# The expert layer of a float32 model in eleven blocks of 128 routed tokens, with the tokens stationary and the weights moving

## The chip, the cores and the metric

The kernel runs on one core of a Trainium2 chip. TensorE multiplies matrices, VectorE (DVE) and ScalarE (ACT) work on vectors, SyncE (SP) issues most DMAs. Each engine takes its instructions in order; semaphores tie the engines together. The metric is the time of one execution on the device in microseconds (us), as the median of several runs.

## The reference

The reference runs a two-layer hybrid mixer model and a two-layer diffusion trunk one after the other, all in float32, on 256 tokens of width 1024 (and 256 context tokens in the second half). The change touches one part alone, the mixture of experts in the second layer of the first half:

```python
def moe_swiglu(h, router_w, w1, w3, w2):
    logits = (h @ router_w).astype(F32)
    top_v, top_i = lax.top_k(logits, TOP_K)                 # TOP_K = 2
    probs = jax.nn.softmax(top_v, axis=-1)
    gates = jnp.sum(jax.nn.one_hot(top_i, N_EXPERTS, dtype=F32) * probs[..., None], axis=-2)
    out = jnp.zeros_like(h)
    for e in range(N_EXPERTS):                              # N_EXPERTS = 8
        out = out + gates[..., e:e + 1] * swiglu(h, w1[e], w3[e], w2[e])
    return out                                              # w1, w3: 1024 x 1408, w2: 1408 x 1024
```

Each of the 256 tokens picks two of eight experts, so the layer needs 512 token-expert pairs, while computing every expert for every token makes 2048. `swiglu(h, w1, w3, w2)` is `(silu(h @ w1) * (h @ w3)) @ w2`.

## The kernel before

The residual X lies in SBUF with features on partitions (8 tiles of 128 features x 256 tokens). A float32 product is made of three float32r passes: every operand is split into a high part (rounded to float32r) and a low part (the rest), and `passes()` (lines 606 to 608) does high*high, high*low and low*high into one PSUM bank. ACT makes the high part of a weight tile (line 1173), DVE the low part (line 1576). Products whose operands are plain float32 (the router, the spreading of one row over all partitions) are single calls; the program turns each into two instructions, a high and a low one, so the trace has two records for each.

A feed-forward layer is a loop (`ffn`, line 719) whose turn has 30 units. Units 0 to 21 make 128 hidden features each (8 tiles of the input width, three passes each, weights stationary, 256 tokens moving); units 22 to 29 make 128 output features each (11 hidden tiles, three passes). For the experts the loop has eight turns, one for each expert, over all 256 tokens, and the output of a turn is multiplied by the expert's gates (`expert_gates`, line 1683) before it goes into X (line 1640). Beside it each turn makes 3 column tiles of the second half's modulation (lines 634 and 641: 8 calls of 384 columns and 3 of 2 columns, which are 16 and 6 records).

Weights go through three raw buffers (`RAW`, filled by SP in `load_ffn`, 1 MB or 1.4 MB each) and three split buffers (`WS`). SP issues the load of a raw buffer when the split of its last contents is done; ACT splits unit n when PE has done unit n-3. All orders are written out by hand, engine by engine, and the waits are semaphore waits in the code.

Ahead of the expert loop stand the norm, the split of the normed h (`norm_apply`), the router (PE line 986), the top two and their softmax (DVE lines 1985 to 1998), and the spreading of the gates over all partitions (PE line 997, DVE line 2003). During this the weights of the first units are already in SBUF. Behind the loop stand the final norm of the first half and the norm of the second half's first layer.

## Time and profile before

| what | value |
|---|---|
| median of the runs | 3401.73 us (3401.4 to 3408.96, three runs) |
| the profiled execution, its own time | 3409.84 us |
| its span, first to last instruction | 3408.1 us |
| granted TensorE clock, mean over the span | 0.966 |
| PE busy, share of the span | 94% |
| DVE busy, ACT busy | 46%, 38% |
| DMA, mean over the span | 150 GB/s, 512 MB |

The span is cut into 40 slices of 85 us on the page. PE is busy in nearly all of them, and the chain of waits that ended last runs over PE for 87% of the span. A busy PE is no PE at its peak: the records of matmuls overlap, so what one costs in a stream is read from the distance between the starts of two neighbours, not from its duration.

### The profile page before, as it was taken

How to read it: one execution, taken by the hardware profiler on the slowest of the kernel's cores; microseconds unless marked ns; L12 is line 12 of the kernel's file. 1: busy time of each engine (PE TensorE's matmuls, PEld its weight loads, DVE VectorE, ACT ScalarE, POOL GpSimd, SP SyncE). 2: the span in 40 equal slices, each digit the busy share in tenths (PEclk: the TensorE clock that was granted, in tenths of full speed). 3: DMA queues.
4: the chain of work that ended last, by engine and by line, in shares of the span. 5: the costliest groups of instructions: out<-in, count | busy, mean ns of one | idle time of the engine just before them, and what ended most of it. 6: DMA issues, size and time to landing. Idle time of an engine off the chain costs nothing.

```text
span 3408.1 us, 53358 instructions
## 1 busy us (share of the span) xinstructions
PE 3200.0 (94%) x20698; PEld 2771.3 (81%) x20698; DVE 1563.7 (46%) x2328; ACT 1308.2 (38%) x1942; POOL 0.2 (0%) x4
## 2 busy tenths in 40 slices
PE   7998989899999999998999999999999999989899
PEld 5887888789999999996777777778777777777798
DVE  4553446545555555554232345533334232346555
ACT  4353343533444434444222244432223222245444
POOL 0000000000000000000000000000000000000000
PEclk8999999889999999998999999999999999999899
DMA  8748764346666666563635322144452545522454
GB/s 298 238 127 263 198 198 136 100 123 181 187 180 198 182 172 186 178 188 109 205 87 170 126 59 75 50 122 132 112 154 75 168 136 155 171 63 87 114 176 133
DMA packets 680961, 512.09 MB, mean 150 GB/s; under 512 B 14795, under 2 KB 674702, under 8 KB 680598
## 3 DMA queue, kind: packets, MB, share of 16 engines
q1 hardware_dynamic: 601510, 390.56, 39.4%
q10 hardware_dynamic: 79216, 118.01, 10.9%
q8 instruction: 195, 3.19, 0.4%
q14 instruction: 40, 0.33, 0.0%
HBM read 507.46 MB, written 1.05 MB: 149 GB/s over the span
## 4 chain that ended last, share of the span: by engine, by line
PE 87%; ACT 5%; DVE 3%; issue 2%; DMA 2%; SPq 1%; ACTq 0%; DVEq 0%
PE bank L606 26%; PE bank L608 25%; PE bank L607 25%; PE bank L634 3%; ACT ring L1227 2%; DMA ada_halves<-in_ada_w 1%; PE bank L641 1%; PE bank L1125 1%; PE bank L1116 1%; ACT weights_split L1173 1%; DVE weights_split L1576 1%; PE bank L1137 1%; ACT hn_split L1226 1%; ACT hn_split L1234 1%; PE bank L690 0%
## 5 line engine op out<-in xcount | busy, mean ns | idle before, releaser
L606 PE MATMUL bank<-hn_split,weights_split 128*128 128x256 f32 (+1 forms) x3888 | 1281.2, 330 | 104.7 <-issue 37.3
L607 PE MATMUL bank<-hn_split,weights_split 128*128 128x256 f32 (+1 forms) x3888 | 1252.4, 322 | 0.0
L608 PE MATMUL bank<-hn_split,weights_split 128*128 128x256 f32 (+1 forms) x3888 | 1251.7, 322 | 0.0
L1576 DVE TENSOR_TENSOR weights_split<-weights_raw,weights_split 128x1024 fp32r<-128x1024 f32 (+2 forms) x670 | 873.2, 1304 | 275.5 <-ACT weights_split L1173 272.6
L1173 ACT ACTIVATE weights_split<-weights_raw 128x1024 fp32r<-128x1024 f32 (+2 forms) x670 | 748.1, 1118 | 603.0 <-PE bank L608 583.9
L606 PEld LDWEIGHTS bank<-hn_split,weights_split 128*128 128x128 f32 x3888 | 757.0, 195 | 238.1 <-issue 139.0
L607 PEld LDWEIGHTS bank<-hn_split,weights_split 128*128 128x128 f32 x3888 | 757.6, 195 | 65.8 <-issue 18.0
L608 PEld LDWEIGHTS bank<-hn_split,weights_split 128*128 128x128 f32 x3888 | 756.8, 195 | 52.2
L1662 DVE TENSOR_TENSOR ring<-ring,bank 128x256 f32<-128x256 f32 (+1 forms) x198 | 101.0, 510 | 998.4 <-PE bank L608 874.9
L606 PE MATMUL bank<-hidden_split,weights_split 128*128 128x256 f32 (+1 forms) x1584 | 508.6, 321 | 0.0
L607 PE MATMUL bank<-hidden_split,weights_split 128*128 128x256 f32 (+1 forms) x1584 | 505.1, 319 | 0.0
L608 PE MATMUL bank<-hidden_split,weights_split 128*128 128x256 f32 (+1 forms) x1584 | 505.0, 319 | 0.0
L1262 ACT ACTIVATE hidden_split<-ring 128x256 fp32r<-128x256 f32 (+1 forms) x198 | 96.9, 490 | 606.3 <-DVE ring L1662 606.2
L606 PEld LDWEIGHTS bank<-hidden_split,weights_split 128*128 128x128 f32 x1584 | 302.5, 191 | 32.4 <-issue 11.9
L608 PEld LDWEIGHTS bank<-hidden_split,weights_split 128*128 128x128 f32 x1584 | 302.5, 191 | 20.9
L607 PEld LDWEIGHTS bank<-hidden_split,weights_split 128*128 128x128 f32 x1584 | 302.6, 191 | 19.8
L1259 ACT ACTIVATE ring<-bank 128x256 f32<-128x256 f32 (+1 forms) x198 | 90.0, 454 | 470.6 <-PE bank L608 470.2
L1640 DVE SCALAR_TENSOR_TENSOR residual<-bank,half_gate,residual 128x256 f32<-128x256 f32 x112 | 49.8, 480 | 232.3 <-PE bank L608 232.2
L1672 DVE TENSOR_TENSOR hidden_split<-ring,hidden_split 128x256 fp32r<-128x256 f32 (+1 forms) x198 | 100.5, 508 | 0.0
L1200 ACT ACTIVATE ring<-residual 128x256 f32<-128x256 f32 (+1 forms) x160 | 73.9, 464 | 48.6 <-DVE residual L1640 43.6
L634 PE MATMUL bank<-ada_halves,cond_second_padded 128*32 128x384 f32 x768 | 81.8, 498 | 0.0
L1600 DVE TENSOR_TENSOR rstd<-rstd,ring 128x256 f32<-128x256 f32 (+1 forms) x144 | 71.6, 497 | 3.9 <-ACT ring L1200 3.3
(300 smaller groups left out, 1957.2 us busy)
## 6 DMA issues: line engine op xcount, KB each, us to landing
weights_raw<-in_moe_w SPq DMA_DIRECT2D x176, 512.0 KB, 5.2
weights_raw<-in_w_ffn_in SPq DMA_DIRECT2D x176, 512.0 KB, 5.1
ada_halves<-in_w_ada ACTq DMA_DIRECT2D x96, 768.0 KB, 4.8
ada_halves<-in_ada_w ACTq DMA_DIRECT2D x54, 768.0 KB, 4.9
weights_raw<-in_w_in SPq DMA_DIRECT2D x60, 512.0 KB, 4.9
weights_raw<-in_moe_w SPq DMA_DIRECT2D x32, 768.0 KB, 4.5
weights_raw<-in_w_ffn_out SPq DMA_DIRECT2D x32, 768.0 KB, 4.6
weights_raw<-in_ffn_w SPq DMA_DIRECT2D x44, 512.0 KB, 5.5
```

What stands on the lines that cost most here:

```text
L606: mm(ps, wh, xh, start=first, stop=False)
L607: mm(ps, wh, xl, start=False, stop=False)
L608: return mm(ps, wl, xh, start=False, stop=last)
L634: i = mm(PS[bank][32 * j:32 * j + 32, 0:ADA_COLS], condp[:, 4 * h + j, :], AH[:, h, j, :], start=h == 0, stop=h == 1)
L1173: act.activation(split_view(slot, 0, kts, n), raw, ACT.Copy).then_inc(split_high, 1)
L1200: act.activation(square_tile(m, T)[:, seg], X[:, m, 0:T][:, seg], ACT.Square).then_inc(square_ready, 1)
L1259: act.activation(RING[:, 0, 0:T], PS[0][:, 0:T], ACT.Silu).then_inc(drained[0], 1)
L1262: act.activation(gs(0, T)[:, f, :], RING[:, 1, 0:T], ACT.Copy).then_inc(g_high, 1)
L1576: tt(split_view(slot, 1, kts, n), raw, split_view(slot, 0, kts, n).bitcast(F32), ALU.subtract)\
L1600: tt(RS[:, 0:T], RS[:, 0:T], square_tile(m, T), ALU.add).then_inc(square_added, 1)
L1662: tt(RING[:, 1, 0:T], RING[:, 0, 0:T], PS[1][:, 0:T], ALU.mult).then_inc(drained[1], 1)
L1672: tt(gs(1, T)[:, f, :], RING[:, 1, 0:T], gs(0, T)[:, f, :].bitcast(F32), ALU.subtract)\
```

## The change

The expert layer leaves the loop. The router gives each token its two experts; a counting step with small matmuls gives each token-expert pair a slot so that each expert owns whole blocks of 128 slots. Eleven blocks always suffice (`MOE_BLOCKS = (2*256 - 8)//128 + 8`), and eleven are always computed. For each block:

- `gather`: 32 float32r matmuls of 128 columns with 0/1 selection matrices (`PICK`) pick the block's tokens out of token rows and leave them with features on partitions; ACT and DVE split them (`XB`).
- `up`: 16 units of one row tile (128 input features) of w1 or w3, all 1408 columns moving, in chunks of 512, 512 and 384, with the block's 128 tokens stationary. Three passes each. The units alternate between w1 (banks 0 to 2) and w3 (banks 3 to 5).
- `turn`: silu on ACT, the product on DVE, 11 PE transposes, copies by ACT. Between the first four transposes and the rest stands `scatter` of the block before.
- `down`: 11 hidden tiles by two halves of 512 output columns in plain float32 (no split), the hidden tile stationary, w2 moving from its own buffers (`W2R`, four pairs of row tiles). Inside it stand the sum of the slots' gates and the next block's `gather`.
- `scatter`: 16 float32r matmuls of 256 columns put the gated result back to token columns, and DVE adds it to X, eight adds for each block.

The expert's number is read by SP from SBUF for each block, and the weight loads take their address from it. The whole is written out, eleven times, with no loop on any engine. All weights of a block are loaded for the block: 17.3 MB, also where two blocks have one expert or a block is empty.

```diff
+MOE_BLOCKS = (2 * SEQ - EXPERTS) // P + EXPERTS
+UP_CHUNKS = ((0, 512), (512, 512), (1024, 384))
+            def load_experts():                                     # SP
+                def up_tile(b, k):
+                    kk = KT * b + k
+                    sp.wait_ge(split_both, MOE_U + 2 * max(0, kk - 2))
+                    r, s = slice(k * P, (k + 1) * P), (MOE_B + kk) % 3
+                    sp.dma_start(RAW[:, s, 0:FFN_GROUP], a["moe_w1"][0][expert[b]][r, :]).then_inc(raw_full[s], 16)
+                    sp.dma_start(RAW[:, s, FFN_GROUP:], a["moe_w3"][0][expert[b]][r, :]).then_inc(raw_full[s], 16)
+                def down_pair(b, j):
+                    n, q = DOWN_PAIRS * b + j, min(2, GT - 2 * j)
+                    if n >= W2_PAIRS:
+                        m = n - W2_PAIRS
+                        sp.wait_ge(S["moe_down"], GT * (m // DOWN_PAIRS) + min(2 * (m % DOWN_PAIRS) + 2, GT))
...
+                sp.wait_ge(S["moe_routed"], BLOCKED)
+                for b in range(MOE_BLOCKS):
+                    expert[b] = sp.value_load(BLOCK_EXPERT[0:1, b:b + 1], min_val=0, max_val=EXPERTS - 1)
+                    up_tile(b, 0)
+                    if b:
+                        down_pair(b - 1, 4)
+                        down_pair(b - 1, 5)
...
-            load_ffn("ffn1.1")
+            load_experts()
+            def experts():                                          # PE
+                def gather(b):
+                    pe.wait_ge(S["moe_picked"], 2 * (b + 1))
+                    for half in range(2):
+                        for k in range(4 * half, 4 * half + 4):
+                            for n in range(4):
+                                t, part = n // 2, n % 2
+                                i = mm(PS[half][:, k % 4 * P:(k % 4 + 1) * P], HROW[:, part, t, k * P:(k + 1) * P],
+                                       PICK[b % 2][:, t, :], start=n == 0, stop=n == 3)
...
+                def up(b):
+                    for v in range(UP_UNITS):
+                        n, k, w = UP_UNITS * b + v, v // 2, v % 2
...
+                        pe.wait_ge(split_both, MOE_U + n + 1)
+                        for c, (c0, cn) in enumerate(UP_CHUNKS):
+                            ps = PS[3 * w + c][:, 0:cn]
+                            xh, xl = (XB[b % 2][:, part, k, :] for part in (0, 1))
+                            wh, wl = (up_split(n, part)[:, c0:c0 + cn] for part in (0, 1))
+                            mm(ps, xh, wh, start=k == 0, stop=False)
+                            mm(ps, xl, wh, start=False, stop=False)
+                            i = mm(ps, xh, wl, start=False, stop=k == KT - 1)
...
+                def scatter(b, banks):
+                    pe.wait_ge(S["moe_y_split"], 2 * (b + 1))
+                    pe.wait_ge(S["moe_placed"], b + 1)
+                    for q in range(4):
+                        if q >= 2 and banks[q] == banks[q - 2]:
+                            pe.wait_ge(x_updated, x0 + KT * b + 2 * (q - 1))
...
+                for b in range(MOE_BLOCKS):
+                    up(b)
+                    turn(b)
+                    down(b)
+                scatter(MOE_BLOCKS - 1, (2, 3, 0, 1))
...
+                def split_up(n):                                    # ACT; DVE makes the low part
+                    block = MOE_B + n // 2
+                    act.wait_ge(raw_full[block % 3], 32 * (block // 3 + 1))
+                    act.wait_ge(unit_done, MOE_U + n - 2)
+                    act.activation(up_split(n, 0), up_raw(n), ACT.Copy).then_inc(split_high, 1)
...
-                            if moe:
-                                tmp = RING[:, 2 + m % 2, 0:T]
-                                dve.wait_ge(x_updated, g * 8 + (x0 + m - 1))
-                                tt(tmp, src[:, 0:T], GATES[:, g, :], ALU.mult).then_inc(gated, 1)
-                                dve.wait_ge(gated, g * 8 + (4 + m + 1))
-                                residual(m, 0, tmp, gate(m, 0), g * 8 + (x0 + m - KT + 1))
...
+                for b in range(MOE_BLOCKS):                         # DVE
+                    for v in range(3, UP_UNITS):
+                        split_up(UP_UNITS * b + v)
+                    if b + 1 < x.n_turns:
+                        add_modulation(b + 1)
+                    for c, (c0, cn) in enumerate(UP_CHUNKS):
+                        dve.wait_ge(S["moe_silu"], 3 * b + c + 1)
...
+                        tt(HID[:, c0:c0 + cn], HID[:, c0:c0 + cn], PS[3 + c][:, 0:cn], ALU.mult).then_inc(S["moe_hidden"], 1)
+                    if b + 1 < MOE_BLOCKS:
+                        pick(b + 1)
+                    if b:
+                        for k in range(KT):
+                            dve.wait_ge(S["moe_scattered"], 4 * (b - 1) + k // 2 + 1)
+                            residual(k, 0, PS[2 + k // 2 % 2][:, k % 2 * SEQ:(k % 2 + 1) * SEQ], gate(k),
+                                     x0 + KT * (b - 2) + k + 1 if b > 1 else None)
+                    if b + 1 < MOE_BLOCKS:
+                        split_up(UP_UNITS * (b + 1))
+                        block_low(b + 1)
+                        split_up(UP_UNITS * (b + 1) + 1)
+                        split_up(UP_UNITS * (b + 1) + 2)
+                    place(b)
```

PE before, inside a turn, from the last pass of the hidden features to the first two products of the output (weights_split is the stationary tile; 128x256 is what moves):

```order
L608 MATMUL bank<-hn_split,weights_split 128x256
L735 ISA
L612 REGISTER_ALU
L616 REGISTER_ALU
L606 MATMUL bank<-hidden_split,weights_split 128x256
L607 MATMUL bank<-hidden_split,weights_split 128x256
L608 MATMUL bank<-hidden_split,weights_split 128x256
```

The hidden features are ready for the next product as they stand, so nothing lies between the two halves of a turn.

PE in the changed kernel, from the last passes of block 1's `up` (lines 901 to 903) to the first of block 2's. block_split is the block's tokens, block_pick and block_place the selection matrices of gather and scatter, block_hidden the hidden rows, block_out_split the block's result; the numbers are those of the two buffers:

```order
L903 MATMUL bank<-weights_split,block_split_114 128x384
L929 MATMUL bank<-tables,block_hidden 128x128 x4
L945 MATMUL bank<-block_place_122,block_out_split 128x256 x16
L929 MATMUL bank<-tables,block_hidden 128x128 x7
L955 MATMUL bank<-expert_down,block_hidden_turned 128x512 x10
L965 MATMUL bank<-small,block_pick_125 128x1 x2
L955 MATMUL bank<-expert_down,block_hidden_turned 128x512 x2
L880 MATMUL bank<-block_pick_124,token_rows_split 128x128 x32
L955 MATMUL bank<-expert_down,block_hidden_turned 128x512 x10
L901 MATMUL bank<-weights_split,block_split_113 128x512
```

Transposes, scatter and gather are new on PE; the down products are 22 calls in place of 264 passes of half the width.

SP before, where the expert loop begins (one raw buffer is filled by two DMAs of 128x8x128):

```order
L557 UNCONDITIONAL_BRANCH
L557 ISA
L564 ISA
L564 DMA weights_raw<-in_moe_w 128x8x128
L565 DMA weights_raw<-in_moe_w 128x8x128
L561 REGISTER_ALU
```

SP in the changed kernel, where block 1 begins:

```order
L654 TENSOR_LOAD block_expert
L654 ISA x2
L639 ISA
L639 DMA weights_raw<-in_moe_w 128x1408
L640 DMA weights_raw<-in_moe_w 128x1408
L649 ISA
L649 DMA expert_down<-in_moe_w 128x2x1024
L649 ISA
L649 DMA expert_down<-in_moe_w 128x1024
L639 ISA
L639 DMA weights_raw<-in_moe_w 128x1408
L640 DMA weights_raw<-in_moe_w 128x1408
```

The loads of w2 (line 649) stand in the one queue between those of w1 and w3 (lines 639 and 640), so that the second row tile of a block is issued behind two loads that wait for the block before to use its w2.

## Rows read from the trace of the kernel before

**Rows 1.** The page: span, busy time, the chain's shares by engine.
```profile
span 3408.1 us, 53358 instructions
PE 3200.0 (94%) x20698; PEld 2771.3 (81%) x20698; DVE 1563.7 (46%) x2328; ACT 1308.2 (38%) x1942; POOL 0.2 (0%) x4
...
PE 87%; ACT 5%; DVE 3%; issue 2%; DMA 2%; SPq 1%; ACTq 0%; DVEq 0%
```

**Rows 2.** Busy time in stretches of the expert layer; columns as the header says.
```profile
core 0: us, PE busy (x) PEld busy (x) DVE busy (x) ACT busy (x) POOL busy (x), PEclk, DMA share, GB/s
640.00:706.00 66.00, 47.04 (x285) 43.44 (x284) 34.77 (x84) 26.36 (x45) 0.00 (x0) 0.72 0.29 81
...
914.00:1018.00 104.00, 98.68 (x815) 96.53 (x816) 57.10 (x78) 43.75 (x61) 0.00 (x0) 1.00 0.65 186
```

**Rows 3.** Timeline of PE at both ends of the loop: start, duration, line, [idle before].
```profile
707.36 0.55 PE L606 MATMUL bank<-hn_split,weights_split 128*128 128x256 f32 x1 [1.88 <-DVE cond_second_padded L1727]
707.71 0.41 PE L607 MATMUL bank<-hn_split,weights_split 128*128 128x256 f32 x1
707.92 0.41 PE L608 MATMUL bank<-hn_split,weights_split 128*128 128x256 f32 x1
...
1533.67 0.50 PE L682 MATMUL bank<-tables,rstd 128*128 128x2 f32 x4
```

**Rows 4.** Timeline of PE at the edge of two turns.
```profile
810.27 0.36 PE L606 MATMUL bank<-hn_split,weights_split 128*128 128x256 f32 x1 [1.59 <-issue]
814.88 0.28 PE L606 MATMUL bank<-hn_split,weights_split 128*128 128x256 f32 x1 [2.58 <-issue]
```

**Rows 5.** Timeline of PE: neighbouring float32r passes of 256, then of 512 columns.
```profile
636.03 0.28 PE L606 MATMUL bank<-hn_split,weights_split 128*128 128x256 f32 x1
636.15 0.28 PE L607 MATMUL bank<-hn_split,weights_split 128*128 128x256 f32 x1
...
1640.04 0.39 PE L608 MATMUL bank<-hn_split,weights_split 128*128 128x512 f32 x1
...
1641.40 0.39 PE L608 MATMUL bank<-hn_split,weights_split 128*128 128x512 f32 x1
```

**Rows 6.** Plain float32 calls: one line's records (ns, first to last start), and timeline.
```profile
L882 PE MATMUL bank<-ret_out,tables x4: 590/592/594, 598.9 to 600.2; 128*128 128x512 f32 x4
...
2105.58 2.08 PE L1116 MATMUL bank<-mla_k,mla_q 96*128 96x512 f32 x4
2107.49 1.06 PE L1125 MATMUL bank<-mla_sum_diagonals,mla_probs 128*128 128x128 f32 x8
2108.48 1.09 PE L1137 MATMUL bank<-mla_probs_t,mla_v 128*64 128x128 f32 x16
```

**Rows 7.** Transposes: one line's records (ns, first to last start).
```profile
L800 PE MATMUL bank<-tables,context_rows x16: 272/272/332, 57.7 to 59.4; 128*128 128x128 f32 x16
```

**Rows 8.** Groups of instructions by form, whole span: busy us, mean ns, idle before.
```profile
L1576 DVE TENSOR_TENSOR weights_split<-weights_raw,weights_split 128x1408 fp32r<-128x1408 f32 x144 | 233.9, 1624 | 51.7 <-ACT weights_split L1173 51.6
L1173 ACT ACTIVATE weights_split<-weights_raw 128x1408 fp32r<-128x1408 f32 x144 | 198.1, 1376 | 282.6 <-PE bank L608 281.8 <-issue 0.6
L634 PE MATMUL bank<-ada_halves,cond_second_padded 128*32 128x384 f32 x768 | 81.8, 498 | 0.0
L1259 ACT ACTIVATE ring<-bank 128x512 f32<-128x512 f32 x66 | 39.4, 597 | 243.0 <-PE bank L608 243.0
L1662 DVE TENSOR_TENSOR ring<-ring,bank 128x512 f32<-128x512 f32 x66 | 45.4, 688 | 540.6 <-PE bank L608 504.0 <-ACT ring L1259 36.6
L1640 DVE SCALAR_TENSOR_TENSOR residual<-ring,mod_first,residual 128x256 f32<-128x256 f32 x64 | 31.0, 485 | 6.5
```

**Rows 9.** DMA: a stretch of pure loading (columns of rows 2), and time to landing.
```profile
15.00:25.00 10.00, 7.00 (x38) 3.30 (x42) 2.52 (x7) 3.57 (x7) 0.00 (x0) 0.66 1.05 387
...
weights_raw<-in_moe_w SPq DMA_DIRECT2D x176, 512.0 KB, 5.2
```

**Rows 10.** Timeline ahead of the loop: last add to X, norm, router, top two.
```profile
665.53 0.48 DVE L1640 SCALAR_TENSOR_TENSOR residual<-bank,mod_first,residual 128x256 f32<-128x256 f32 x1 [0.16 <-PE bank L608]
...
677.88 13.82 PE L986 MATMUL bank<-router_w,hn_split 128*128 128x8 f32 x64 [8.98 <-DVE hn_split L1622]
```

**Rows 11.** Timeline of DVE at the loop's end: the last add to X.
```profile
1534.42 0.48 DVE L1640 SCALAR_TENSOR_TENSOR residual<-ring,mod_first,residual 128x256 f32<-128x256 f32 x1
```

**Rows 12.** A small DVE operation of 128 columns: one line's records.
```profile
L2150 DVE TENSOR_SCALAR mla_sum_diagonals<-tables,small x48: 285/286/290, 2101.9 to 3149.8; 128x128 f32<-128x128 f32 x48
```

More of the change, by code:

```diff
@@ L345, in program @@
             phase(f"ffn1.{layer}")
-            loop_blocks(2 if layer == 0 else EXPERTS)
+            if layer == 0:
+                loop_blocks(2)
+            else:
+                for n in range(KT * MOE_BLOCKS):
+                    blocks.append(None)
+                    units.extend([(len(blocks) - 1, None, None, None, None)] * 2)
         for layer in range(DEPTH):
@@ L1710, in out_phase @@
                 for u in range(u0, u1):
[L1711 removed]
+                    ahead(u, u1 + (0 if name in ("out1.1", "out2.1") else 2))
                     m = u - u0
```

477 lines of the change are left out of this document (382 added, 95 removed).

## The prediction

> **What bounds the kernel now.** I read the page first: over the whole span PE is busy for 94%, and the chain that ended last runs over PE for 87% [rows 1]. DVE (46%) and ACT (38%) are covered by it. The second view is the busy time by stretches. In one turn of the expert loop PE is busy for 98.7 of 104 us at a granted clock of 1.00, DVE for 57, ACT for 44, and the DMA engines for 0.65 at 186 GB/s [rows 2]. So the layer costs what its stream of passes on PE costs, until something else is put in its way. The timeline of PE gives its length: the first product starts at 707.36 and the norm behind the last one at 1533.67, so 826.3 us for eight turns, 103.3 each [rows 3]. Neighbouring passes of 256 columns start 0.120 us apart [rows 5], and a turn has 22 x 8 x 3 + 8 x 11 x 3 = 792 of them: 95.0 us. The modulation beside them costs 8 x 2 records of 384 columns (on 32 of the array's columns; 16 records busy 81.8 / 768 x 16 = 1.7 us [rows 8]) and six small ones, some 0.7, so 2.4 us. At the edge of two turns PE stands still for 1.59 and 2.58 us on "issue" [rows 4], 4.2 us. That is 101.6 of 103.3.
>
> **The price of a pass in the changed shape.** A float32r pass of 512 columns costs (1641.40 - 1640.04) / 6 = 0.227 us [rows 5], less than two of 256. For 384 columns there is no row; I take the middle of 0.120 and 0.227, 0.174. A plain float32 call of 512 columns is two records, and four records of line 882 start within 1.3 us, 0.43 apart; four of line 1116 take 1.91 us to the next line's start, 0.478 each [rows 6]. So a call costs 0.86 to 0.96 us, and I take 0.86, from the line with 128 rows and 128 columns, as here. Transposes: 16 in 1.7 us of starts, 0.113 [rows 7].
>
> **One block on PE.**
> - up: 16 units x (6 x 0.227 + 3 x 0.174) = 16 x 1.88 = 30.1 us.
> - turn: 11 transposes x 0.12 = 1.3; scatter 16 x 0.12 (256-column passes) = 1.9.
> - down: 22 x 0.86 = 18.9 us (bound above 22 x 0.96 = 21.0). In float32r it would be 66 passes x 0.227 = 15.0, so this part of the change costs PE 4 us per block and spares ACT and DVE the splits.
> - the gates' sum, four records: 0.5.
> - gather: 32 passes of 128 columns. No row shows a float32r pass so narrow. From below: eight float32 records of 128 columns start in 0.99 us, 0.12 each [rows 6], the same as a float32r pass of 256, so something beside the columns keeps records 0.12 apart. From above: float32 takes two records, 0.24. I take 0.12, the nearest in kind (one record each): 3.8 us; the other end is 7.7.
>
> **What PE waits for in a block.** In turn PE waits inside scatter. DVE has to do the three products of the hidden rows (0.69, 0.69, 0.55), the four selections (0.29 each [rows 12]) and then the adds to X (0.48 each [rows 8]), and scatter's third pair needs the first two adds, since it reuses banks 2 and 3. Counted from the end of up: products done at 0.95, selections at 2.1, two adds at 3.1, third pair 3.2 to 3.7, two more adds at 4.1, fourth pair to 4.7, seven transposes to 5.5. PE's own work in it is 3.2, so 2.3 to 2.4 us of idle; silu (0.6 each, as line 1259 [rows 8]) is hidden by the last unit, because it starts on w1's banks a unit earlier. At the end of down no wait is left: the next unit 0 uses other banks, and its 1.88 us cover the split of the result (0.6 + 0.7 behind the last half), for which unit 1 waits.
>
> Split weights: a unit of 1408 columns costs ACT 1.376 and DVE 1.624 [rows 8]. DVE alone could feed one unit in 1.68; the ring of three gives a period of (1.38 + 1.62 + 0.35 of hand-overs + 1.88) / 3 = 1.74. Both are under PE's 1.88, so PE keeps the lead, with little to spare. The one thing in ACT's way is the issue of two modulation loads (some 1 us) in seven blocks; I give it 4 us in all.
>
> Raw weights: a block loads 3 x 1024 x 1408 x 4 bytes = 17.3 MB. The trace's stretch of pure loading ran at 387 GB/s with the engines full [rows 9]: 44.6 us, and the block is 58.9. The average fits, the order does not quite. A row tile of w1 and w3 is 1.44 MB, 3.7 us at 387; the loop now lands 2 x 0.5 MB 5.2 us after issue [rows 9], of which the bytes are 3.7 at 186 / 0.65 = 286 GB/s, so some 1.5 us are latency, and a tile lands 5.2 to 5.9 us after its two issues. Issue waits for the split of the tile three before. Landing to both splits done takes 1.38 + 2 x 1.62 + 0.3 = 4.9. So three tiles pass in 10.1 to 10.8, and PE takes 11.3 for three. Into this the queue puts w2's fourth pair (1.05 MB, 2.7 us) behind tile 5, and tiles 6 and 7 come some 2.5 us late. I take 2 us per block, between 0 and 5.
>
> A block: 30.1 + 3.2 + 2.4 + 18.9 + 0.5 + 3.8 = 58.9, with the loads 60.9. Eleven: 670. Less the first scatter and last gather (5.7), plus 7 modulation parts of 2.4 (17) and ACT's 4: 685. The loop was 826.3: -141 us. With it go 264 passes a turn in down, the 33 us of issue at turn edges, and DVE's gate products, which were covered.
>
> The Trainium skill, page "DMA: Bandwidth & Descriptors", section "Where 436 GB/s comes from", gives a core some 358 GB/s from HBM as the side that binds. This case's stretch went faster, 387, so the measurement decides; by the page a block's loads take 48.3 us and the late tiles grow by about 1.4 us a block, 15 us in all.
>
> **Ahead of the blocks.** The last add to X starts at 665.53 and the first product at 707.36 [rows 3, 10]. What goes: the split of h, 64 router records at 0.216 (13.8 us [rows 10]), the spreading of the gates. What comes: h, 16 transposes and 32 router records, some 10.4 us at that rate, to 680; top two for both halves at once, 2.5; counting matmuls and seven small DVE steps to the experts' numbers, about 687; and only then may SP read and load, a row tile after 6 to 7 us. Meanwhile slots, selections, gather(0) at the slow rate (7 us), its splits, and the first weight split: first product about 701.5, and the splits of units 1 to 3 stand in one queue with other DVE work, 2 us more. I take -4 us, between -10 and +8. The loads, ready in advance before, are hidden behind gather.
>
> **Behind them.** Before, the last add to X started 0.75 us after PE's next work [rows 11]. Now, after the last down: the split of the result 1.6, two splits for the next layer on DVE 2.5, then eight adds and seven sums of squares in turn, 7 us. That is 11 for 1.3: +10.
>
> Sum: -141 - 4 + 10 = -135. The profiled execution took 3409.8 us (span 3408.1), which gives 3275; it lies 8 above the median of 3401.7. On the median: 3267 us.
>
> **Rivals.**
> - R1, the narrow passes of gather cost as float32: +0.12 x 32 = 3.8 us in ten blocks, 38: 3305. For it: the passes are of a width that no row has. Against: one record should not cost two.
> - R2, late tiles cost 5 us a block, not 2 (the queue's waits on moe_down add up): +33, 3300. For it: 10.8 against 11.3 leaves half a us in a cycle.
> - R3, the idle of turn drops the clock. At half clock a pass of 256 costs 0.21 [rows 3]. For it: PE pauses in every block's turn. Against: after pauses of 1.59 and 2.58 us the next pass at 814.88 had the full-clock duration of 0.28 [rows 4]. If it fell in each block and three to five us of down ran at half speed, +30: 3297. The Trainium skill's "TensorE: Matmul & The Clock Gate", section "HAM oscillation — how this bites in real kernels", says that kernels with thin M, waiting for DMA between short bursts, fall to the half clock again and again; this block of 128 tokens is such a shape, and the trace agrees only for the longer idle ahead of 707.36.
> - R4, slower than before: the loads pace the blocks. The turn before moved 186 GB/s [rows 2]; if one in-order queue with its waits on moe_down got no more, a block would take 17.3 / 0.186 = 93 us and the kernel 3267 + 11 x 32 = 3619. It decides from the block time that eats the gain, 60.9 + 135 / 11 = 73.2 us, 236 GB/s. Against: 387 was reached, the engines' share now is 0.65, and a queue of 1.4 MB requests has a tile or two in flight.
> - R5, better than said: no late tiles and half the idle in turn, -22 - 13: 3232.
>
> **Numbers.** Forecast 0.50 (own range 3240 to 3290), R1 0.22, R2 0.12, R3 0.04, R5 0.08, R4 0.04. Range 3228 to 3322: R1, R2, R3 and R5 with their spread; out of it stay R4 and the cases where R1 and R2 meet. What a measurement of this kernel can tell from no change is about 0.3%, 10 us. All but R4 are faster by far more: faster 0.95, same 0.01, slower 0.04.
>
> **What would show it.** Starts of 512-column passes in up 0.227 apart; plain float32 records in down 0.43 apart; a block every 60 to 61 us; gather 3.8 us long (R1: 7.7); idle before PE in turn of 2 to 3 us behind DVE's adds; idle in up behind the splits of the last four row tiles and ACT waiting there for DMA (none: R5; 5 us: R2); clock 1.00 through the blocks; DMA near 280 GB/s. Wrong would be a block over 66 us, or an up in which ACT waits for DMA in most units.

## The result, and the profile of the changed kernel

Timed side by side on one chip, the kernel before took 3401.57 us (3396.39 to 3408.96) and the changed one 3268.61 us (3265.63 to 3276.25): ratio 0.9611 with a 95% interval of 0.9587 to 0.9635, so 133 us less. The profiled execution of the changed kernel took 3276.25 us, its span is 3274.5.

The page of the changed kernel, the lines that answer to [rows 1], and the loads of the row tiles (us to landing at the end):

```profile
span 3274.5 us, 44218 instructions
...
PE 3065.1 (94%) x17103; PEld 2467.9 (75%) x17103; DVE 1506.4 (46%) x2152; ACT 1265.9 (39%) x1769; POOL 0.2 (0%) x4
...
PE 79%; ACT 6%; DMA 6%; DVE 5%; issue 2%; SPq 1%; ACTq 0%; DVEq 0%
...
weights_raw<-in_moe_w SPq DMA_DIRECT2D x176, 704.0 KB, 7.4
```

The share of busy time on PE is the same 94%, and only the chain tells the two profiles apart: PE had 87% of it [rows 1] and has 79%, and DMA went from 2% to 6%. PE is still the engine that bounds the kernel, but the loads now reach it at some places. PE runs 3595 records fewer.

Busy time by stretches (columns as in [rows 2]), first all eleven blocks, then the 104 us that [rows 2] show of before:

```profile
697.00:1386.00 689.00, 653.34 (x2867) 467.31 (x2867) 383.96 (x405) 298.58 (x299) 0.00 (x0) 0.99 0.75 288
914.00:1018.00 104.00, 98.22 (x431) 67.70 (x432) 54.64 (x66) 40.87 (x45) 0.00 (x0) 1.00 0.73 283
```

In the same 104 us PE has 431 records where it had 815, and is as full as before; the DMA engines move 283 GB/s instead of 186. In the blocks as a whole PE is idle for 689.0 - 653.3 = 35.7 us, 3.2 a block. What it waits for is in the waits of that stretch (in total us, times, longest):

```profile
ACT weights_split L1532 <- DMA weights_raw<-in_moe_w: 65.8, 32, 3.5
PE bank L901 <- DVE weights_split L2036: 24.1, 20, 2.3
PE bank L945 <- DVE residual L1943: 12.7, 10, 1.4
```

The 24.1 us hold one wait that is no late tile: the layer's first product waits 1.89 us at 697.03, and does so in every run below. Two causes remain: the split of a late row tile (19 times, 22.2 us, 2.0 a block) and scatter's third pair, which waits for the first adds to X (ten times, 1.27 each). ACT waits much longer for the loads than PE does for the splits; most of its 65.8 us costs nothing.

The timeline of PE from the end of one up to the gather and beyond (start, duration, line, [idle before]) shows a block's other parts in a row:

```profile
795.28 0.60 PE L929 MATMUL bank<-tables,block_hidden 128*128 128x128 f32 x4
795.64 1.20 PE L945 MATMUL bank<-block_place,block_out_split 128*128 128x256 f32 x8
798.19 1.52 PE L945 MATMUL bank<-block_place,block_out_split 128*128 128x256 f32 x8 [1.36 <-DVE residual L1943]
799.56 0.92 PE L929 MATMUL bank<-tables,block_hidden 128*128 128x128 f32 x7
800.32 8.75 PE L955 MATMUL bank<-expert_down,block_hidden_turned 128*128 128x512 f32 x20
808.91 0.50 PE L965 MATMUL bank<-small,block_pick 128*128 128x1 f32 x4
809.27 1.96 PE L955 MATMUL bank<-expert_down,block_hidden_turned 128*128 128x512 f32 x4
810.67 4.09 PE L880 MATMUL bank<-block_pick,token_rows_split 128*128 128x128 f32 x32
814.59 8.80 PE L955 MATMUL bank<-expert_down,block_hidden_turned 128*128 128x512 f32 x20
```

The turn takes 800.32 - 795.28 = 5.04 us, of which 1.36 is idle. Twenty records of down start in 808.91 - 800.32 = 8.59, 0.43 each. The 32 narrow passes of gather take 814.59 - 810.67 = 3.92, 0.1225 each. Behind this pause the passes run at full speed.

Behind some of the late tiles they don't. This is block 2, in the timeline of PE and in the columns of [rows 2]:

```profile
850.29 0.51 PE L901 MATMUL bank<-weights_split,block_split 128*128 128x512 f32 x1 [1.37 <-DVE weights_split L2036]
...
851.45 0.63 PE L901 MATMUL bank<-weights_split,block_split 128*128 128x512 f32 x1
851.87 0.63 PE L902 MATMUL bank<-weights_split,block_split 128*128 128x512 f32 x1
```

```profile
850.70:854.00 3.30, 3.30 (x10) 2.81 (x9) 1.82 (x2) 1.39 (x2) 0.00 (x0) 0.50 1.02 404
```

Passes of 512 columns start 0.43 apart there, and the granted clock is 0.50, the lower of the two levels (1.2 and 2.4 GHz). The same happens behind the waits of 1.91 us at 1167.54 and of 1.82 us at 1348.61, each time for 3.4 us, in which half of the work is done; I estimate 1.7 us lost each time, 5 in all. Behind none of scatter's ten waits did the clock fall.

A unit of up, from its first pass to that of the next:

```profile
1206.70 0.40 PE L901 MATMUL bank<-weights_split,block_split 128*128 128x512 f32 x1
1206.94 0.39 PE L902 MATMUL bank<-weights_split,block_split 128*128 128x512 f32 x1
...
1208.09 0.34 PE L901 MATMUL bank<-weights_split,block_split 128*128 128x384 f32 x1
1208.27 0.34 PE L902 MATMUL bank<-weights_split,block_split 128*128 128x384 f32 x1
...
1208.62 0.40 PE L901 MATMUL bank<-weights_split,block_split 128*128 128x512 f32 x1
```

It takes 1.92 us: six passes of 512 columns in 1208.09 - 1206.70 = 1.39, 0.232 each (the first 0.24), and three of 384 in 0.53, 0.177 each.

How a late tile reaches PE stands in the chain of waits of one block, in order of time (start, us, what):

```profile
1214.64 1.40 ACT weights_split L1532
1216.06 1.64 DVE weights_split L2036
1217.87 0.34 SPq L639
1218.28 0.34 issue
1218.62 8.79 DMA weights_raw<-in_moe_w
1227.43 1.39 ACT weights_split L1532
1228.85 1.64 DVE weights_split L2036
1230.53 0.50 PE bank L901
```

From the split of a place's w3 half to that of the next tile's w1 half in it are 12.8 us (1214.64 to 1227.43), 8.8 of them a load that was forecast at 5.2 to 5.9. The split of the old tile's w1 half had started a unit earlier, at 1212.72, so the whole cycle of the place is 14.7 us. PE takes three tiles in 6 x 1.92 = 11.5. Where this cycle stands in the way, PE waits.

The DMA engines are full while it happens (columns as in [rows 2]):

```profile
1200.00:1232.00 32.00, 29.72 (x126) 22.94 (x125) 21.32 (x16) 17.52 (x14) 0.00 (x0) 1.00 0.96 375
1232.00:1248.00 16.00, 14.60 (x69) 10.76 (x68) 11.05 (x19) 5.94 (x9) 0.00 (x0) 1.00 0.07 27
```

The 288 GB/s over all blocks are the mean of stretches in which everything is asked for at once and of others in which the queue waits for a buffer. In the first of these two stretches, row tiles and w2 share all that the engines move. It is no exception: ahead of the late tiles of blocks 2, 3 and 5 (840 to 855 us, 905 to 918, 1030 to 1047) the engines' share is 1.02 and 404 to 410 GB/s are moved.

The last two places are the ends of the layer. Ahead of the blocks (timelines of DVE, SP and PE):

```profile
662.61 0.48 DVE L1943 SCALAR_TENSOR_TENSOR residual<-bank,mod_first,residual 128x256 f32<-128x256 f32 x1 [1.48 <-PE bank L711]
...
683.51 0.37 SPq L639 DMA_DIRECT2D weights_raw<-in_moe_w  x1
...
686.24 7.09 PE L880 MATMUL bank<-block_pick,token_rows_split 128*128 128x128 f32 x32 [4.62 <-DVE token_rows_split L2012]
...
697.03 0.76 PE L901 MATMUL bank<-weights_split,block_split 128*128 128x512 f32 x1 [1.89 <-DVE weights_split L2036]
```

And behind them:

```profile
1387.61 2.17 PE L945 MATMUL bank<-block_place,block_out_split 128*128 128x256 f32 x16 [1.56 <-DVE block_out_split L2135]
...
1387.74 2.36 DVE L1879 TENSOR_TENSOR weights_split<-weights_raw,weights_split 128x1024 fp32r<-128x1024 f32 x2 [0.19 <-ACT weights_split L1401]
...
1398.24 0.48 DVE L1943 SCALAR_TENSOR_TENSOR residual<-bank,mod_first,residual 128x256 f32<-128x256 f32 x1
1398.38 1.01 PE L785 MATMUL bank<-tables,rstd 128*128 128x2 f32 x4 [8.60 <-DVE rstd L1903]
```

From the last add of the layer before to the first product it is 697.03 - 662.61 = 34.4 us; before it was 41.8 [rows 3, 10]. The products of the blocks end at about 1386.0, so the blocks take 689.0 where the loop took 826.3. From their end to the last add it is 12.2 us, where it was 0.75 [rows 11], and PE stands still for 8.60 of them.

At the last add the gain is 1534.42 - 1398.24 = 136.2 us: 2.9 that the layer starts earlier, 7.4 ahead of the blocks, 137.3 in them, less 11.4 behind them. The rest of the kernel gives 2.6 back, which is within what executions of one kernel differ by. So are the first 2.9: in the traces of the changed kernel and its variants below, the last add of the layer before starts between 661.2 and 666.2, and at 660.88 in that of run 1, whose code is the kernel before up to there.

### The profile page after: what moved, and what is told of

The parts are those of the page before. It is cut to its first block, busy times and chain, and to the rows that moved or that the text cites. A ratio compares the mean times of both kernels' runs of the same rounds, so it can differ in the third digit from the quotient of the medians.

```text
span 3274.5 us, 44218 instructions
## 1 busy us (share of the span) xinstructions
PE 3065.1 (94%) x17103; PEld 2467.9 (75%) x17103; DVE 1506.4 (46%) x2152; ACT 1265.9 (39%) x1769; POOL 0.2 (0%) x4
## 4 chain that ended last, share of the span: by engine, by line
PE 79%; ACT 6%; DMA 6%; DVE 5%; issue 2%; SPq 1%; ACTq 0%; DVEq 0%
PE bank L709 19%; PE bank L711 18%; PE bank L710 18%; PE bank L955 6%; DMA weights_raw<-in_moe_w 4%; PE bank L737 3%; PE bank L901 2%; ACT ring L1455 1%; PE bank L903 1%; PE bank L902 1%; DVE weights_split L2036 1%; DMA ada_halves<-in_ada_w 1%; PE bank L880 1%; PE bank L744 1%; PE bank L1353 1%
## 5 line engine op out<-in xcount | busy, mean ns | idle before, releaser
L709 PE MATMUL bank<-hn_split,weights_split 128*128 128x256 f32 (+1 forms) x2480 | 876.8, 354 | 69.4 <-DVE hn_split L1925 30.1
L710 PE MATMUL bank<-hn_split,weights_split 128*128 128x256 f32 (+1 forms) x2480 | 852.9, 344 | 0.0
L711 PE MATMUL bank<-hn_split,weights_split 128*128 128x256 f32 (+1 forms) x2480 | 852.4, 344 | 0.0
L1879 DVE TENSOR_TENSOR weights_split<-weights_raw,weights_split 128x1024 fp32r<-128x1024 f32 (+1 forms) x430 | 554.2, 1290 | 250.7 <-ACT weights_split L1401 247.4
L1401 ACT ACTIVATE weights_split<-weights_raw 128x1024 fp32r<-128x1024 f32 (+1 forms) x430 | 475.6, 1108 | 456.8 <-PE bank L711 444.9
L709 PEld LDWEIGHTS bank<-hn_split,weights_split 128*128 128x128 f32 x2480 | 485.8, 196 | 201.0 <-issue 111.2
L711 PEld LDWEIGHTS bank<-hn_split,weights_split 128*128 128x128 f32 x2480 | 485.3, 196 | 52.2
L710 PEld LDWEIGHTS bank<-hn_split,weights_split 128*128 128x128 f32 x2480 | 486.4, 196 | 49.9 <-issue 1.9
L2036 DVE TENSOR_TENSOR weights_split<-weights_raw,weights_split 128x1408 fp32r<-128x1408 f32 x176 | 283.1, 1624 | 134.1 <-ACT weights_split L1532 134.0
L709 PE MATMUL bank<-hidden_split,weights_split 128*128 128x512 f32 (+1 forms) x880 | 308.6, 351 | 0.0
L710 PE MATMUL bank<-hidden_split,weights_split 128*128 128x512 f32 (+1 forms) x880 | 305.1, 347 | 0.0
L711 PE MATMUL bank<-hidden_split,weights_split 128*128 128x512 f32 (+1 forms) x880 | 305.1, 347 | 0.0
L1532 ACT ACTIVATE weights_split<-weights_raw 128x1408 fp32r<-128x1408 f32 x176 | 239.5, 1379 | 134.7 <-PE bank L903 68.5
L901 PE MATMUL bank<-weights_split,block_split 128*128 128x512 f32 x528 | 209.3, 396 | 24.2 <-DVE weights_split L2036 24.1
L955 PE MATMUL bank<-expert_down,block_hidden_turned 128*128 128x512 f32 x484 | 214.4, 595 | 0.0
L903 PE MATMUL bank<-weights_split,block_split 128*128 128x512 f32 x528 | 200.8, 380 | 0.0
L902 PE MATMUL bank<-weights_split,block_split 128*128 128x512 f32 x528 | 199.3, 378 | 0.0
L709 PEld LDWEIGHTS bank<-hidden_split,weights_split 128*128 128x128 f32 x880 | 166.6, 189 | 32.4 <-issue 11.3
L711 PEld LDWEIGHTS bank<-hidden_split,weights_split 128*128 128x128 f32 x880 | 166.6, 189 | 20.9
L710 PEld LDWEIGHTS bank<-hidden_split,weights_split 128*128 128x128 f32 x880 | 166.7, 189 | 19.8
```

The lines of the kernel that those rows point to most:

```text
L709: mm(ps, wh, xh, start=first, stop=False)
L710: mm(ps, wh, xl, start=False, stop=False)
L711: return mm(ps, wl, xh, start=False, stop=last)
L901: mm(ps, xh, wh, start=k == 0, stop=False)
L902: mm(ps, xl, wh, start=False, stop=False)
L903: i = mm(ps, xh, wl, start=False, stop=k == KT - 1)
```

## The experiments

Every ratio below is against the kernel before, timed on the same chip. Between runs of the changed kernel and its variants I compare these ratios; 0.001 of them is 3.4 us.

**1. Only the loop written out, in the kernel before.** The change also writes eleven blocks out where a hardware loop stood. This run gives the kernel before that form, and nothing else.

```diff
+        def turns_of(engine, n, name):
+            if name == "ffn1.1":
+                yield from range(n)
+            else:
+                with engine.Fori(0, n) as g:
+                    yield g
...
-                with pe.Fori(0, turns) as g:
+                for g in turns_of(pe, turns, name):
```

> The kernel before, with the eight turns of its expert loop written out on all engines and nothing else changed. Theory (a part of the gain is the code form, not the blocks): PE stood still for 1.59 and 2.58 us on issue at each of seven turn edges, 29 us in all; written out, this goes, so about 3401.6 - 29 = 3373 us (3365 to 3380). Rival (these waits are the fetching of instructions or stand for some other wait that comes late anyway): 3398 to 3405 us.

Measured: 3370.71 us, ratio 0.9901 (0.9879 to 0.9923), so 33 us less. The waits of PE from 700 to 1500 us, first of the kernel before, then of this one:

```profile
PE bank L606 <- issue: 28.9, 14, 2.6
```

```profile
PE bank L689 <- DVE rstd L1607: 5.5, 1, 5.5
PE bank L613 <- DVE cond_second_padded L1734: 1.4, 1, 1.4
```

The idle time on issue is gone to the last of its 14 places, and with it as much time as the seven edges of [rows 4] said, and some 4 us more. Those 4 are of the size of what the clock cost at the edges. In the kernel before, it fell behind three of the seven, and at the first of them right behind the passes of [rows 4] (columns as in [rows 2]):

```profile
815.80:819.00 3.20, 3.20 (x17) 3.20 (x16) 0.00 (x0) 0.00 (x0) 0.00 (x0) 0.50 0.02 5
```

The other two stretches at 0.50 begin at 1228.7 and 1437.0, and in this run the granted clock is 1.00 from 706 to 1490 us. At 1.7 us each, that is an estimated 5 us. So a quarter of the change's 133 us could be had by this form alone. The other 100 are what is left for the routing and the new shape of the products together; no run separates these two.

**2. Eight blocks instead of eleven.** The price of a block, measured by itself.

```diff
-MOE_BLOCKS = (2 * SEQ - EXPERTS) // P + EXPERTS
+MOE_BLOCKS = 8
```

> The changed kernel with 8 blocks in place of 11 (blocks 8 to 10 are left out, and with them the token-expert pairs that they hold). Theory (the layer is a sum of equal blocks, each paced by PE with 1 to 3 us of late tiles): minus three blocks of 61.3 to 62.8 us, 3268.6 - 187 = 3082 us (3075 to 3090), and the spacing of the remaining blocks unchanged. Rival (the first blocks run on loads that are ahead, the cost of a block is set by the loads at 17.3 MB and the loads catch up in the later blocks): another spacing than 61 to 64 us in the blocks that are left.

Measured: 3090.65 us, ratio 0.9070 (0.9045 to 0.9095). Against the changed kernel's 0.9611 three blocks are worth 0.0541 x 3403 = 184 us by ratio, or 180 if the changed kernel is put at 0.9611 x 3403.18 = 3270.8 on this chip and the median taken off: 60 to 61 us a block, the prediction's 60.9 within an error of about 4. The time lies just past the upper end of what was expected (3090). The blocks that are left start 62.9 us apart on the average, the same blocks of the changed kernel 63.1, so the rival, another spacing, fell.

**3. The second weight's loads made small.** Is w2's traffic behind the late tiles, and behind the unit's 1.92 us? After the first round of its ring each load of w2 brings 64 columns instead of 1024; the descriptors are the same in number.

```diff
-                    w = a["moe_w2"][0][expert[b]][2 * j * P:(2 * j + q) * P, :]
+                    cols = D if n < W2_PAIRS else 64
+                    w = a["moe_w2"][0][expert[b]][2 * j * P:(2 * j + q) * P, 0:cols]
-                    sp.dma_start(W2R[:, n % W2_PAIRS, 0:q, :], w.rearrange("(k p) n -> p k n", p=P))\
+                    sp.dma_start(W2R[:, n % W2_PAIRS, 0:q, 0:cols], w.rearrange("(k p) n -> p k n", p=P))\
```

> The changed kernel with the loads of w2 cut to 64 of 1024 columns from the fifth pair on (what is left out is the loading of w2; the down products compute with stale weights), so 12 MB are loaded per block in place of 17.3. Theory (w2's pairs in the queue make the last row tiles late, 22 us of idle PE before up's units in all, and nothing else hangs on the loads): 3268.6 - 22 = 3247 us, idle of PE behind DVE's splits 0 to 3 us, ACT no longer waiting for DMA. Rival A (the unit of up that costs 1.95 us in place of 1.88 is slowed by the DMA traffic too): 12 us more, 3235 us, with 1.88 per unit. Rival B (the late tiles come from the ring of three row tiles alone, landing plus splitting): no change, 3265 to 3272 us.

Measured: 3259.06 us, ratio 0.9574 (0.9553 to 0.9594), 12 us less, halfway between the theory and rival B. PE's wait, and the landing of the row tiles:

```profile
PE bank L902 <- DVE weights_split L2037: 12.6, 13, 2.1
...
weights_raw<-in_moe_w SPq DMA_DIRECT2D x176, 704.0 KB, 5.9
```

The bytes of w2 are half of the cause: they stretch the landing from 5.9 to 7.4 us, and half of PE's wait goes with them (22.2 us become 10.7 without the first product's 1.9). The other half stays when the tiles land in the 5.9 us that I had forecast. A unit takes 1.92 here too (1206.02 to 1207.94), so its 0.04 above the forecast has nothing to do with w2's traffic, and rival A fell.

**4. Down in float32r.** Each plain float32 call becomes three float32r passes of 512 columns, on operands that are split already.

```diff
-                            i = mm(PS[4 + h][:, :], HIDT[:, f, :], W2R[:, m % W2_PAIRS, f % 2, h * 512:(h + 1) * 512],
-                                   start=f == 0, stop=f == GT - 1)
+                            x, w = XB[b % 2][:, 0, f % KT, :], HROW[:, 0, f % 2, h * 512:(h + 1) * 512]
+                            mm(PS[4 + h][:, :], x, w, start=f == 0, stop=False)
+                            mm(PS[4 + h][:, :], x, w, start=False, stop=False)
+                            i = mm(PS[4 + h][:, :], x, w, start=False, stop=f == GT - 1)
```

> The changed kernel with each plain float32 call of down replaced by three float32r passes of 512 columns over tiles that lie in SBUF anyway (the down product is left out, its waits stay; no splits are added). It prices float32 against three passes. Theory (a float32 call is two records 0.43 us apart, three passes are 3 x 0.227 us, and PE is the bound): 11 x 22 x (0.86 - 0.68) = 43 us less, 3226 us. Rival (the shorter down leaves the loads of the next block less time, so late tiles take the gain back): 3240 to 3260 us, with more idle of PE behind the splits than 22 us.

Measured: 3233.38 us, ratio 0.9497 (0.9469 to 0.9525), 37 us less, or 3.4 a block with an error of about 1. In the trace the part of a block from the last transpose to the second unit of the next block takes 21.1 us instead of 24.9, 3.9 less in each, and the starts of the blocks are 58.78 apart instead of 62.74, 3.96 less. PE waits for the splits as long as before:

```profile
PE bank L901 <- DVE weights_split L2038: 25.0, 21, 1.8
```

The price of float32 in down stands nearly as the prediction worked it out: 3.9 us a block in the trace. The rival, that a shorter down lets the loads fall behind and gives half of it back, fell. What the splits of w2 and of the turned hidden would cost ACT and DVE is not in this run, and a kernel with both wasn't tried.

**5. The changed kernel again**, as the measure for the next three, on their chip.

> The changed kernel as it is, on the chip of the three that follow, so that they can be compared with it: 3262 to 3275 us.

Measured: 3274.23 us, ratio 0.9617 (0.9600 to 0.9635), the same as the first time. PE's wait for splits is 23.5 us in this trace.

**6. w2's fourth pair behind the block's last row tile.** The prediction put the late tiles down to this pair, which stands in the queue ahead of tiles 6 and 7.

```diff
                     up_tile(b, 5)
-                    down_pair(b, 3)
                     up_tile(b, 6)
                     up_tile(b, 7)
+                    down_pair(b, 3)
```

> The changed kernel with w2's fourth pair of a block issued behind row tiles 6 and 7 in SP's queue, not ahead of them. Theory (this pair, 1.05 MB, makes tiles 6 and 7 late): of the 22 us of idle PE before units of up, 10 to 20 go, so 3249 to 3259 us. Rival B (the cycle of the ring, landing plus splitting, makes them late): within 5 us of the changed kernel's time.

Measured: 3262.18 us, ratio 0.9585 (0.9567 to 0.9603), 12.0 us less than run 5.

```profile
PE bank L901 <- DVE weights_split L2036: 14.8, 14, 2.4
```

PE's wait of 23.5 us in run 5 became 14.8, or 21.6 became 12.9 without the first product's. The pair's place is a cause, but not the only one, just as its bytes were in run 3.

**7. Scatter into four banks.** The third and fourth pair go to banks 0 and 1 instead of again 2 and 3; gather then waits for the adds of the block before.

```diff
+                    if b > 1:
+                        pe.wait_ge(x_updated, x0 + KT * (b - 1))
...
-                            scatter(b - 1, (2, 3, 2, 3))
+                            scatter(b - 1, (2, 3, 0, 1))
...
-                            residual(k, 0, PS[2 + k // 2 % 2][:, k % 2 * SEQ:(k % 2 + 1) * SEQ], gate(k),
+                            residual(k, 0, PS[(2, 3, 0, 1)[k // 2]][:, k % 2 * SEQ:(k % 2 + 1) * SEQ], gate(k),
```

> The changed kernel with scatter inside turn spread over banks 2, 3, 0, 1 in place of 2, 3, 2, 3; gather waits for the adds that read banks 0 and 1. Theory (scatter's second half waits 1.35 us for DVE's adds only because it reuses the banks): 12.7 us of idle go, 3256 us. Rival (the wait moves to gather or to the transposes, or the loads, which had this time to catch up, come later by as much): less than 5 us gained.

Measured: 3257.46 us, ratio 0.9567 (0.9551 to 0.9583), 16.8 us less than run 5. PE's wait for the adds is gone; what is left:

```profile
PE bank L903 <- DVE weights_split L2038: 20.5, 20, 2.1
```

The 12.7 us of the wait came back and a little more (PE's wait for splits is 3.0 us shorter too), and nothing behind them took their place. The rival fell.

**8. Runs 6 and 7 in one kernel**, to see whether the two gains add up.

> Both of these changes together. If they are independent the gains add: about 3268.6 - 15 - 13 = 3241 us. If the time saved in turn only makes the row tiles later, the sum is less than the two gains, about 3250.

Measured: 3248.36 us, ratio 0.9538 (0.9519 to 0.9557), 25.9 us less than run 5, where the two had 28.8 together. Within the error, some 10 us for such a difference, the gains add. PE's wait for splits is 11.9 us.

**9. The halves of a row tile wait one by one.** A tile's place in the ring has a half for w1 and one for w3. The changed kernel loads both when both are split; here w1's half is loaded as soon as w1's is. This shortens the ring's cycle by one split, and leaves w2 alone.

```diff
-                    sp.wait_ge(split_both, MOE_U + 2 * max(0, kk - 2))
+                    sp.wait_ge(split_both, MOE_U + max(0, 2 * (kk - 3) + 1))
                     sp.dma_start(RAW[:, s, 0:FFN_GROUP], a["moe_w1"][0][expert[b]][r, :]).then_inc(raw_full[s], 16)
+                    sp.wait_ge(split_both, MOE_U + 2 * max(0, kk - 2))
                     sp.dma_start(RAW[:, s, FFN_GROUP:], a["moe_w3"][0][expert[b]][r, :]).then_inc(raw_full[s], 16)
```

> The changed kernel with the load of w1's half of a row tile issued as soon as the split of w1's unit three tiles before is done, one unit earlier than now; w3's half waits as before. It tests the other half of the late tiles: cutting w2's loads left 12.6 of 24.1 us of idle PE behind the splits. Theory (the ring's cycle, landing plus splitting, makes them late, and w1's bytes a unit earlier shorten the landing of a tile by up to 1.8 us): 8 to 15 us less than the changed kernel, a ratio to before near 0.958, with 8 to 14 us of this idle left. Rival (bandwidth alone makes them late, the same bytes in the same time): within 4 us of the changed kernel.

Measured: 3258.09 us, ratio 0.9569 (0.9547 to 0.9591), by ratio 14 to 16 us less than the changed kernel, more than the rival's 4.

```profile
PE bank L902 <- DVE weights_split L2037: 13.2, 10, 2.5
```

The ring's cycle has a share of the late tiles. Neither the pair nor the cycle does it alone: each of them removed leaves 11 to 13 us, the first product's wait not counted.

**10. All three edits (6, 7 and 9).**

> All three edits together (w2's fourth pair last, four banks for scatter, w1's half issued a unit earlier). If the causes of the late tiles are the pair and the ring and each has its own share, the idle behind the splits falls from 24 us to under 8, and the time is 6 to 12 us under that of the first two together (3248 us): 3236 to 3242 us. Rival (the pair and the ring are one shortage, already relieved): 3244 to 3250 us.

Measured: 3227.72 us (3224.35 to 3228.42), ratio 0.9474 (0.9455 to 0.9493), faster than was expected. By ratio it is 22 us under run 8, where 6 to 12 were forecast. The two traces differ by 14.5 us (spans of 3237.9 and 3223.4): 9.7 are PE's waits for splits, and some 3.4 by my estimate two stretches at the low clock behind late tiles in run 8, of which run 10 has none in its blocks. What is left of the 22 is within the error. It is the fastest kernel of this study, 1.4% under the changed one and 5.3% under the kernel before. The waits in its blocks, and its busy time in two stretches:

```profile
ACT weights_split L1535 <- DMA weights_raw<-in_moe_w: 9.3, 9, 2.1
...
PE bank L904 <- DVE weights_split L2039: 2.2, 2, 1.9
```

```profile
697.00:1350.00 653.00, 642.04 (x2885) 464.36 (x2883) 394.62 (x423) 308.27 (x310) 0.00 (x0) 0.99 0.81 307
914.00:1018.00 104.00, 104.00 (x467) 72.49 (x466) 59.95 (x64) 48.29 (x48) 0.00 (x0) 1.00 0.84 318
```

PE has no idle time in the second stretch. Its blocks start 56.65 us apart, or 59.36 where modulation stands beside them. With the pair's place and the cycle both mended, 2.2 us of PE's wait for splits are left, and 1.9 of them are the layer's first product: the late tiles are down to 0.3 us. One at a time they leave 12.9 and 11.3, and the pair with the four banks (run 8) 10.0. Either of the two was enough to keep some of the tiles late, which is why none of the single edits took much more than half. The bytes are the same 17.3 MB a block, so what made the tiles late can be mended by when they are asked for. In the first stretch above the DMA engines' share is 0.81, where the changed kernel has 0.76 from 697 to 1350 us.

## Why the prediction held

The forecast sum was 135 us, and 136 were found at the last add. It came out closer than its terms: several were off by 3 to 10 us, with both signs, and the errors cancelled. That closeness is luck. The mechanism, a stream of passes on PE with a few named waits, is what the runs bear out; one mechanism that the prediction had ruled out, the clock, was at work as well.

- **Up.** Forecast 1.88 a unit and 30.1 a block; measured 1.92, and 30.7 (16 x 1.92) to 31.0 (a block late in the layer, its wait taken off). Run 10, in which up hardly waits, has 31.0; in both kernels the first unit of a block takes 2.3, and 0.4 of it is the end of down's last product (run 4, without float32, has 1.88). A pass of 512 columns took 0.232 on the average of a unit, not 0.227, one of 384 took 0.177, not 0.174. Over the eleven blocks that is 7 us, or 10 with the 0.4. Its cause is not settled; run 3 excludes w2's traffic.
- **Turn.** Forecast 3.2 of work and 2.4 of idle time, 5.6; measured 5.04, 6 us less over ten blocks. The idle time that the profile counts is 1.36. The third pair came nearly where it was forecast, 2.9 behind the end of up (3.2 said); what follows it was shorter, since DVE's adds start 0.41 apart (seven steps in 2.89 us), not 0.48, and so the fourth pair hardly waits. Run 7 shows that the wait is scatter's two banks, as said.
- **Down, gates, gather.** Forecast 18.9 + 0.5 + 3.8 = 23.2; 22.9 in a block late in the layer. Records of 0.43 [rows 6] held, from a line elsewhere in the kernel with the same shape, and run 4 bears out the 4 us that float32 costs here, with 3.9 in the trace. R1 fell: 128 columns of float32r start 0.1225 apart, one record each.
- **Late tiles.** Forecast 2 us a block, measured 2.0. The size was right and the cause half of it, so the match is luck. I had put it to w2's fourth pair alone, with a ring that just kept up (10.8 against 11.3 for three tiles). But landing took 7.4 us, not 5.2 to 5.9: with the 4.9 of the splits that is 12.3, over PE's 11.5, and the one cycle followed above took 14.7. The forecast took the time to landing from a loop in which the engines' share was 0.65; here it is 0.96 while the row tiles come. R2 was this mechanism at 5 us a block; it was there, at less than half of that. What the forecast left out is that PE can come back from such a wait at half clock, 0.5 us a block more in this trace.
- **A block.** Forecast 58.9 without late tiles; run 10's late blocks, which have none, are 56.65 apart, and with the 1.9 that four banks take off a turn that makes 58.6. With the late tiles 60.9 was forecast. The starts of blocks are 62.7 apart on the average, six of the ten distances with modulation, and 62.1 in the four without; those four hold two of the three stretches at the low clock. Run 2 gives 60 to 61. The eleven took 689 us in this trace, and 684 in that of run 5, the same kernel; the forecast was 685.
- **Ahead.** Forecast -4, measured -7.4, inside the bounds. The last add of the attention part comes at 662.61 instead of 665.53; other traces spread by more than that, so it can't be put down to the change.
- **Behind.** Forecast +10, measured +11.4. The chain of the split, two splits for the next layer and eight adds with their sums stands in the rows as it was counted, the last part with 8.2 us (1390.0 to 1398.24) instead of 7.
- **R3, the clock.** The prediction gave it 0.04, and it was there in part, in another place. The granted clock is 0.99 over the blocks and 1.00 in the stretch of 104 us, but it fell to 0.50 behind three waits for late tiles, for 3.4 us each. Scatter's pause of 1.36 us in turn, which R3 had named, never did it; other waits for late tiles of 1.51 and 1.68 us (at 725.93 and 1042.28) didn't either, so the length of one pause does not decide it. The argument against R3 was misread: the pass at 814.88 had the full-clock duration, but the clock fell at 815.7, some 0.8 us behind it. At 5 us the rival was a sixth of its 30. Ahead of 697.03, behind a router's work at the low level, the passes stay 0.43 apart until about 700.4. The Trainium skill's "TensorE: Matmul & The Clock Gate", section "HAM oscillation — how this bites in real kernels", describes kernels with thin M that wait for DMA between short bursts and fall to the half clock each time; the trace agrees for 3 of the 19 waits for late tiles, and the trace of before did so behind three turn edges, not only ahead of 707.36 as the prediction says.
- **R4, the loads as the pace.** The price that decides was 236 GB/s; 288 were moved in the blocks and 318 in a stretch of run 10, so on the average the loads had room. The Trainium skill, "DMA: Bandwidth & Descriptors", section "Where 436 GB/s comes from", names 358 GB/s from HBM as the side that binds; the measurement went past it, with 375 GB/s over 32 us of a block and 410 over 13 us of another. The 1.4 us a block that the page's figure would have added to the late tiles did not come: they are the 2.0 that was forecast without it. Still, in parts of a block the engines were full, and in the stretches looked at above it is there that the tiles were late.

One part of the gain was named in a single clause: the 33 us of issue at turn edges. Run 1 shows it to be a quarter of the whole, and it belongs to the form of the code. The other 100 are eleven blocks in 689 us against eight turns of 99 (103.3 less the 4.2 at an edge), 793 in all.

## What to carry to other kernels

Price such a change by passes: count them by width, take each width's spacing from anywhere in the trace where the same form stands, and add the few waits by name; here that gave 685 us for a measured 689. Don't count on a ring of buffers that keeps up by less than 10% on paper: here the margin (10.1 to 10.8 against 11.3) was less than what the time to landing grew by with the traffic (5.2 to 7.4). Look at the bandwidth in stretches: 288 GB/s on the average hid stretches of over 400 with the engines full. Where two causes feed one wait, each of them removed alone takes only a part of it (22 us to 12.9 and 11.3 here) and both together nearly all (0.3), so a single edit that gives half of what was expected is a reason to look for the second cause.

## What the runs showed of the hardware

- Float32r passes of 128 columns start 0.1225 us apart, those of 256 columns 0.120: nothing was gained by the narrower pass. 384 columns cost 0.177, 512 columns 0.227 to 0.24.
- The edge of a turn of a hardware loop cost PE about 4.2 us, in two idle times on issue, and behind three of seven edges the clock fell to 0.50 for 3.4 us; written out, the seven edges gave 33 us back (run 1), and PE had no wait on issue in 11 blocks of straight code.
- The time to landing of a 704 KB load hung on what else was in the queue: 7.4 us in the changed kernel, 6.8 in run 10 although more was moved per second, 5.9 in run 3 with w2's loads made small. In stretches of 13 to 17 us ahead of late tiles the engines were full (share 1.02) at 404 to 410 GB/s.
- PE's clock fell to its lower level, granted 0.50 for 3.4 us, behind 3 of 19 waits for late tiles (pauses of 1.37, 1.82 and 1.91 us) and behind none of ten pauses in turn of up to 1.4 us; other waits of 1.51 and 1.68 us left it at 1.00. An estimated 1.7 us is lost each time.
